# Adding up the squares later: GpSimd's additions behind VectorE's residual chain, and the product of ones one weight piece later

## The reference

```python
def second_block(x, norm_g, ...):
    for i in range(DEPTH_2):            # 4 layers
        g = norm_g[i]
        hn = _rms(x, g[0])
        kind = i % N_MIXERS             # conv, pool, attention, conv
        ...
        x = x + _rms(m, g[1])
        f = _swiglu(_rms(x, g[2]), ffn_w_gate[i], ffn_w_up[i], ffn_w_down[i])
        x = x + _rms(f, g[3])
    return x

def _rms(x, g):
    y = xf * lax.rsqrt(jnp.mean(xf * xf, axis=-1, keepdims=True) + EPS)
    return (y * g.astype(jnp.float32)).astype(x.dtype)

def _swiglu(xn, w_gate, w_up, w_down):
    return (jax.nn.silu(xn @ w_gate) * (xn @ w_up)) @ w_down
```

## Time and profile before

| | |
|---|---|
| median of 3 runs | 2614.14 us |
| profiled execution, span | 2612.3 us |
| PE busy | 2443.9 us, 94% |
| DVE busy | 1083.6 us, 41% |
| ACT busy | 673.0 us, 26% |
| POOL busy | 42.5 us, 2% |
| chain that ended last | PE 74%, DMA 14%, DVE 8%, ACT 2% |
| the last four layers | from about 1376 us to the end |

### The profile page before, as it was taken

One profiled execution on the slowest core, in us unless ns is written; L12 is line 12 of the kernel. 1 busy time (PEld: TensorE's weight loads), 2 busy tenths in 40 slices (PEclk: granted clock), 3 DMA queues, 4 the chain that ended last, 5 costly groups with the idle time before them and its releaser, 6 DMA issues.

```text
span 2612.3 us, 38167 instructions
## 1 busy us (share of the span) xinstructions
PE 2443.9 (94%) x15594; PEld 1787.4 (68%) x15594; DVE 1083.6 (41%) x1569; ACT 673.0 (26%) x828; POOL 42.5 (2%) x34
## 2 busy tenths in 40 slices
PE   6899879999999999999998899969999799998998
PEld 4567744444444444444448899959988799988998
DVE  8474231111111111111127655566554465576653
ACT  2121110000000000000014344344443444444432
POOL 0000000000000000000000000000000000000000
PEclk8899879999999999999998999979999899999999
DMA  8265339999999999999993455425544145544542
GB/s 340 98 236 230 139 145 419 422 422 422 422 422 422 422 422 422 422 422 422 422 408 113 146 186 178 176 77 178 183 152 164 65 148 188 179 146 142 181 177 80
DMA packets 93762, 676.40 MB, mean 259 GB/s; under 512 B 10452, under 2 KB 11096, under 8 KB 11640
## 3 DMA queue, kind: packets, MB, share of 16 engines
q1 hardware_dynamic: 92592, 673.36, 65.1%
q10 hardware_dynamic: 1096, 1.97, 0.2%
HBM read 674.23 MB, written 1.06 MB: 259 GB/s over the span
## 4 chain that ended last, share of the span: by engine, by line
PE 74%; DMA 14%; DVE 8%; ACT 2%; issue 1%; SPq 0%; POOL 0%; DVEq 0%; ACTq 0%; POOLq 0%
DMA ring<-in_w_exp 14%; PE psum L456 13%; PE psum L752 13%; PE psum L458 13%; PE psum L457 13%; PE psum L777 5%; PE psum L736 3%; DVE arena L1406 3%; PE psum L627 2%; DVE arena L1412 2%; PE psum L470 2%; PE psum L787 1%; PE psum L527 1%; PE psum L665 1%; DVE arena_parts L1412 1%; DVE x L1406 1%
## 5 line engine op out<-in xcount | busy, mean ns | idle before, releaser
L457 PE MATMUL psum<-arena_parts,ring_parts 128*128 128x256 f32 x2832 | 810.5, 286 | 0.0
L456 PE MATMUL psum<-h_parts,ring_parts 128*128 128x256 f32 x1920 | 555.9, 290 | 38.4 <-DVE arena_parts L1412 37.2
L457 PEld LDWEIGHTS psum<-arena_parts,ring_parts 128*128 128x128 f32 x2832 | 553.8, 196 | 0.2
L458 PE MATMUL psum<-h_parts,ring_parts 128*128 128x256 f32 x1920 | 548.9, 286 | 0.0
L367 DVE TENSOR_TENSOR ring_parts<-ring,ring_parts 128x2048 fp32r<-128x2048 f32 x181 | 414.4, 2291 | 323.6 <-ACT ring_parts L1207 318.8
L752 PE MATMUL psum<-ring,arena 128*64 128x512 f32 x2176 | 487.6, 598 | 5.6 <-DMA ring<-in_w_exp 5.6
L456 PEld LDWEIGHTS psum<-h_parts,ring_parts 128*128 128x128 f32 x1920 | 374.6, 195 | 47.6 <-issue 32.0
L458 PEld LDWEIGHTS psum<-h_parts,ring_parts 128*128 128x128 f32 x1920 | 374.8, 195 | 0.0
L1207 ACT ACTIVATE ring_parts<-ring 128x2048 fp32r<-128x2048 f32 x181 | 342.4, 1903 | 71.7 <-DMA ring<-in_w_mix 47.2
L752 PEld LDWEIGHTS psum<-ring,arena 128*64 128x64 f32 x2176 | 152.4, 137 | 297.7 <-issue 297.6
L1409 DVE TENSOR_SCALAR arena<-psum 128x512 f32<-128x512 f32 x68 | 47.0, 691 | 625.3 <-ACT arena L1186 471.0
(11 more groups left out here) (248 smaller groups left out, 1907.2 us busy)
## 6 DMA issues: line engine op xcount, KB each, us to landing
ring<-in_w_exp SPq DMA_DIRECT2D x408, 1024.0 KB, 19.2
ring<-in_w_ffn SPq DMA_DIRECT2D x132, 1024.0 KB, 4.8
ring<-in_w_mix SPq DMA_DIRECT2D x49, 1024.0 KB, 4.8
ring<-in_w_ada SPq DMA_DIRECT2D x24, 1024.0 KB, 6.4
ring<-in_w_in SPq DMA_DIRECT2D x16, 1024.0 KB, 11.0
ring<-in_w_out SPq DMA_DIRECT2D x4, 1024.0 KB, 4.8
ring<-in_w_attn SPq DMA_DIRECT2D x2, 1024.0 KB, 4.8
ring<-in_w_ssm SPq DMA_DIRECT2D x2, 1024.0 KB, 7.7
```

Source lines behind the costliest of these rows:

```text
L456: mm(out, w[0], a[0], start=start, stop=False, **more)
L457: mm(out, w[0], a[1], start=False, stop=False, **more)
L458: return mm(out, w[1], a[0], start=False, stop=stop, **more)
```

## The change

Two things. GpSimd's four additions now wait until VectorE has made all eight low parts of the stage's input, that is, until the residual chain is through. And PE's product of ones, which was issued behind the first weight piece of the stage, is issued behind the second: in the attention layer, in the two convolution mixers, and in the FFNs (behind up instead of gate). Nothing is computed otherwise.

```diff
             def diff_attention(ready):
                 for n in range(8):
                     late_pair(h2, "qk_read", ready if n == 0 else None)
-                    if n == 0:
+                    if n == 1:
                         x_sums(5)
...
                         last.then_inc(late, 1)
-                        if first and half == 0:
+                        if first and half == 1:
                             x_sums(3)
...
                         late_pair(h2, "stage_read", ready if n == 0 else None)
-                        if n == 0:
+                        if n == 1:
                             x_sums(5)
...
                 if k == 4 * POOL_LAYER + 4:
                     continue
+                pool.wait_ge(sem("late_h_low"), KC * (added + 1))
                 pool.wait_ge(sem("squares_ready"), 4 * k + 2)
                 adds(nc.gpsimd.tensor_tensor(square_sum, squares[:, 0:2, :], squares[:, 2:4, :], ALU.add))
```

## The result

The changed kernel takes 2647.22 us (median of 4 runs, 2646.95 to 2647.66), the kernel before 2613.65 us (4 runs, 2613.1 to 2614.66). The ratio is 1.0129 (95% interval 1.0115 to 1.0143): 33.6 us slower, where +33.1 and 2647 us were forecast. The span of the profiled execution went from 2612.3 to 2645.6 us.

A forecast was written before the change was run, and what follows sets the result against it. PE, busy for 94% of the span, was taken to bound the kernel. Terms -14.6 + 17.4 + 15.6 + 14.7 = +33.1 us on 2614.1 gave 2647 us, own range 2640 to 2655, with rivals 2629 to 2658.

The forecast's parts named there:

- first pieces end sooner: First weight pieces of seven stages: 1.7 us gained in the first mixer, 2.15 in each of six others, -14.6 us.
- mixers, third piece: Mixers of layers 0, 2 and 3: third piece waits for the first result's reader, 5.8 us later each, +17.4 us.
- FFNs, fifth piece: Four FFNs: fifth piece waits for `f_low`, 3.55 us in three and 4.95 us in layer 1, +15.6 us.
- clock behind seven stops: PE behind each of seven new stops: lower granted clock costs 2.1 us each, +14.7 us; bounds nothing and 18.6.
- The additions wait: Start of each stage: GpSimd's additions no longer hold up VectorE's residual chain, -14.6 us; bounds nothing and 21.3 us.
- The product behind the second piece: PE, seven stages: rstd_x comes 5.8 us later, +17.4 us in three mixers and +15.6 us in four FFNs.
- The clock: PE's granted clock falls behind each of seven new stops of 3.6 to 6.2 us, +14.7 us.
- the first rival: PE's seven new stops come but the clock stays up: 2632.5 us; chance 0.18, whole or in some stops.
- The second: VectorE's stretched instructions aren't GpSimd's doing or don't free PE: no gain, costs stay, 2662 us; chance 0.07.
- The third: PE isn't held by the factor, banks and `f_low` being ready in time: 2599.5 us; chance 0.03.

The follow-up runs named there:

- the move alone: Changed kernel without GpSimd's wait, the product of ones still behind the second piece: 2655.20 us, ratio 1.0160.
- the wait alone: Kernel before plus GpSimd's wait, the product of ones staying behind the first piece: 2625.72 us, ratio 1.0047.
- the last experiment: Changed kernel (late place of the product), with VectorE reading each stage's first result before splitting a weight piece: 2607.97 us, ratio 0.9982.
- the product in the middle: Changed kernel with the product of ones ahead of the second piece's fifth block, GpSimd's wait kept: 2616.84 us, ratio 1.0015.
- the filled version: Changed kernel with products of ones with constants in PE's stops, 13 per mixer, 7 per FFN (10 in layer 1): 2632.66 us, ratio 1.0074.
- the version with the middle place and VectorE's new order: Changed kernel, product mid second piece, VectorE reading the first result before splitting a weight piece: 2596.14 us, ratio 0.9937 against before.

## Why the prediction was right

The sum came out at +32.9 us in the stages, where +33.1 was forecast. Each term is within about a microsecond; that the sum is closer still is chance, since a gain 1.0 us too large stands against costs 1.1 us too large:

| term | forecast | trace | from |
|---|---|---|---|
| first pieces end sooner | -14.6 | -13.6 | start of product before, of second piece after |
| mixers, third piece | +17.4 | +17.2 | 11.5 later in sum, plus their gain of 5.7 |
| FFNs, fifth piece | +15.6 | +15.2 | 7.2 later in sum, plus their gain of 8.0 |
| clock behind seven stops | +14.7 | +14.2 | what is left to the seventh piece |

*The additions wait.* Right, and shown by taking the wait away and adding it alone: in sum over the seven stages the first pieces are 12.9 us shorter in the changed kernel than in the move alone (starts of the second piece 57.4 against 70.3 us), and 13.4 us shorter with the wait alone than before (starts of the product 75.9 us, less 18.8 us of stops, against 71.0 us less a wait of 0.5). The first mixer's piece ended at +8.2, where 1392.8 less 1384.7 makes +8.1. The gain was put 1.0 us too large: the seven stages gained 1.6 to 2.3 us, 1.95 in the mean, where the six with three delayed instructions had been put at 2.15. The prediction took 5.2 us of half clock at the start of each stage; six of them had 5.1 to 6.0 us, and the seventh, with the largest gain, 3.4. So the size of this term hangs on the clock: the 53.8 us of the last experiment's first pieces would make the gain 17.2 us.

*The product behind the second piece.* Right in mechanism and size. The chain behind it took 6.43 us in each of the mixers (6.55, 6.44 and 6.44 before), the stops were 5.84 us (6.2 forecast), 3.27 us in three FFNs and 4.67 us in layer 1 (3.6 and 5). From start to start the gaps are 6.43, 3.55 and 4.96 us; the idle of the rows counts from the modelled end of the last matmul.

*The clock.* All seven stops were followed by half clock, and filling them took that away: 13.9 us behind the stops, of the 14.2 found in the trace. The price per stop was 2.3 to 2.4 us in the mixers and in layer 1's FFN and 1.6 us in the three other FFNs, so 2.1 us is right only in the mean. That it was seven of seven is in part luck for the three FFN stops of 3.27 us: in the move alone one of three stops of that length left the clock up, and with the product in the middle one of 2.98 us and one of 2.77 us did.

*The rivals.* The clock stayed up in none of the seven stops, so the first rival is out; its 2632.5 us is near what the filled version takes, 2632.7 us. The second, no gain from the wait, has its own experiment in the move alone: 2655 us rather than 2662, since it kept the first pieces' old length but paid less for the clock. The third, that PE isn't held by the factor, is out by the rows of 5.84 us; its price, 2599.5 us, is near what the version with the middle place and VectorE's new order takes, 2596.1 us.

What the prediction did not see is how cheap the cure is: the 5.8 us were lost to a chain of 6.4 us, of which 4.2 us were ScalarE's copy (1.90 us) and VectorE's low part (2.29 us) of a weight piece that nobody waited for yet.

## What to carry to other kernels

Two engines that hold each other up may be kept apart in time, but then look at what the delayed one feeds: here 2 us a stage were won, and 5.8 us of lateness were put into a chain that already held PE up by 0.3 us in the mixers and had 2.4 us of slack in the first FFN. Before a step is moved later, measure the slack of its first consumer on the busiest engine, and take out of the chain between them what belongs to another. A new stop of PE costs more than its length when the granted clock falls in it, and the share is read from the pace of the matmuls behind it.

## What the runs showed of the hardware

- GpSimd's addition of two 128x512 tensors takes 1.29 us alone. Beside VectorE's instructions with two tensors in SBUF it took 1.45 to 1.52 us in the first mixer, and in the six other stages of the kernel before the second addition took 1.79 to 1.80 us. VectorE's instructions end 0.3 us behind the addition, three of 0.47 us becoming 3.80 us. So both engines lose.
- The granted clock doesn't follow the length of a stop alone. All stops of 3.7 us and more lowered it, in every run. So did the two of 2.37 us (near 1461.5 and 2370 in the kernel before) in every run, and the five of 2.59 to 3.27 us with GpSimd's wait alone. Left at 1.00 it was by stops of 1.50 and 1.79 us (late place, VectorE's new order), of 2.23 and 2.34 us (GpSimd's wait alone: the FFNs of layers 0 and 2), but also by one of 2.77 and one of 2.98 us (product in the middle) and one of 3.26 us (move alone), beside others of about the same length that lowered it. And in the kernel before, a stop of 1.72 us near 2041.7, the seventh of eight waits within 25 us, was followed by a clock of 0.50. What else decides stays open.
- Matmuls of float32 constants, one every 0.44 us, kept the clock at 1.00 over 5.6 us.
